# Moving half of the softmax scaling of some query tiles from GpSimd to VectorE

## The reference, cut to what matters

```
s = einsum('bqhd,bkhd->bhqk', qb, k) * scale
s = where(mask, s, NEG_INF)
p = softmax(s, axis=-1)            # layer one: a sink logit joins the denominator
o = einsum('bhqk,bkhd->bqhd', p, v)
# layer two: o = g[..., 0:1] * o_c + g[..., 1:2] * o_s + g[..., 2:3] * o_w
```

## Time and profile before

| what | value |
|---|---|
| time, median of 3 runs (lowest to highest) | 2753.47 us (2751.24 to 2755.43) |
| the profiled execution: its time | 2746.99 us |
| the profiled execution: span from first to last instruction | 2745.2 us |
| busy over the span | PE 88%, PEld 67%, DVE 58%, ACT 28%, POOL 33% |
| the chain that ended last, by engine | PE 60%, POOL 17%, DVE 14%, ACT 5%, issue 3% |
| mean granted clock of TensorE | 0.919 of full speed |

### The profile page before, as it was taken

How to read it: one execution, slowest core, us unless ns; L and a number is a source line. 1 busy time by engine, 2 the same in 40 slices (tenths; PEclk the granted TensorE clock), 3 DMA queues, 4 the chain that set the end, 5 groups by cost and what they waited for, 6 DMA issues and landing times.

```text
span 2745.2 us, 31261 instructions
## 1 busy us (share of the span) xinstructions
PE 2406.8 (88%) x12233; PEld 1831.3 (67%) x12233; DVE 1591.6 (58%) x2435; ACT 766.2 (28%) x1706; POOL 910.1 (33%) x944
## 2 busy tenths in 40 slices
PE   3968898689999899799879989899799998999978
PEld 2756676468887666676666857476477785747656
DVE  7676684753244665565654457683745536766463
ACT  2233212512001453324322152322311215232311
POOL 2873897378601346852020010400302001030120
PEclk7979898888689899899989989999999999999999
DMA  6440455044543001330111202021121120212111
GB/s 211 136 132 9 115 138 123 1 123 116 137 74 62 17 2 40 116 114 32 62 51 57 69 28 76 29 93 46 46 92 62 62 78 31 62 31 78 61 46 62
DMA packets 229157, 200.27 MB, mean 73 GB/s; under 512 B 86835, under 2 KB 213139, under 8 KB 228755
## 3 DMA queue, kind: packets, MB, share of 16 engines
q1 hardware_dynamic: 217491, 156.33, 20.6%
q0 software_dynamic: 11520, 41.95, 5.3%
HBM read 196.16 MB, written 2.10 MB: 72 GB/s over the span
## 4 chain that ended last, share of the span: by engine, by line
PE 60%; POOL 17%; DVE 14%; ACT 5%; issue 3%; DMA 0%; SPq 0%; DVEq 0%; ACTq 0%; POOLq 0%
PE bank L506 14%; PE bank L507 14%; PE bank L508 14%; POOL mix L2198 6%; POOL mix L2195 4%; PE bank L618 4%; PE bank L654 3%; DVE wring_parts L1496 2%; PE bank L632 2%; POOL mix L2201 2%; POOL mix L2182 2%; PE bank L818 1%; DVE bank L1567 1%; DVE whi_parts L1495 1%; PE bank L572 1%
## 5 line engine op out<-in xcount | busy, mean ns | idle before, releaser
L507 PE MATMUL bank<-h_parts,whi_parts 128*128 128x512 f32 (+2 forms) x1336 | 539.1, 404 | 0.0
L1496 DVE TENSOR_TENSOR wring_parts<-wring,whi_parts 128x2048 fp32r<-128x2048 f32 (+1 forms) x138 | 330.1, 2392 | 4.8
L1495 DVE CAST whi_parts<-wring 128x2048 fp32r<-128x2048 f32 (+1 forms) x138 | 195.1, 1414 | 196.8 <-PE bank L508 158.4
L507 PEld LDWEIGHTS bank<-h_parts,whi_parts 128*128 128x128 f32 (+2 forms) x1336 | 253.8, 190 | 69.9 <-issue 6.0
L2198 POOL TENSOR_TENSOR mix<-mix 128x512 f32<-128x512 f32 (+1 forms) x160 | 216.3, 1352 | 12.5
L506 PE MATMUL bank<-vt_parts,whi_parts 128*128 128x512 f32 (+2 forms) x472 | 199.6, 423 | 18.0 <-POOL h_parts L2229 12.1
L507 PE MATMUL bank<-mix_parts,whi_parts 128*128 128x512 f32 x512 | 204.1, 399 | 0.0
L506 PE MATMUL bank<-pt_parts,whi_parts 128*128 128x512 f32 x392 | 165.5, 422 | 31.1 <-DVE wring_parts L1496 16.2
L508 PE MATMUL bank<-vt_parts,wring_parts 128*128 128x512 f32 (+2 forms) x472 | 190.5, 404 | 0.0
L1567 DVE CUSTOM_DVE_ANT_0 bank<-bank,causal 128x128 f32<-128x128 f32 (+3 forms) x256 | 120.3, 512 | 75.5 <-PE bank L618 75.1
L2195 POOL TENSOR_TENSOR mix<-mix,cond 128x1024 f32<-128x1024 f32 x80 | 161.0, 2013 | 8.7 <-DMA mix<-in_ada_w 7.0
(11 more groups left out here) (372 smaller groups left out, 5347.5 us busy)
## 6 DMA issues: line engine op xcount, KB each, us to landing
wring<-in_w_in SPq DMA_DIRECT2D x60, 1024.0 KB, 5.2
mix<-in_ada_w POOLq DMA_DIRECT2D x80, 512.0 KB, 4.8
wring<-in_w_out SPq DMA_DIRECT2D x16, 1024.0 KB, 5.2
wring<-in_mla_w_in SPq DMA_DIRECT2D x10, 1024.0 KB, 7.1
wring<-in_mla_w_out SPq DMA_DIRECT2D x8, 1024.0 KB, 5.4
wring<-in_swa_w_in SPq DMA_DIRECT2D x32, 256.0 KB, 4.8
wring<-in_nsa_w_in SPq DMA_DIRECT2D x32, 256.0 KB, 4.6
wring<-in_nsa_w_in SPq DMA_DIRECT2D x6, 1024.0 KB, 6.0
```

The costliest lines, as they stand in the source:

```text
L507: pe.matmul(bank, lh, rl, start=False, stop=False)
L1495: chain(dve.tensor_copy(high, whole))
L1496: dve.tensor_tensor(low, whole, high.bitcast(F32), ALU.subtract).then_inc(done, 1)
```

## The change

In the first stack, VectorE now multiplies the second head's row in the steps that `scaled_by_dve` names: i = 3 in layers zero, two and three, and i = 1, 2 and 3 in layer one. GpSimd keeps the first head's row there, and both rows in all other steps. VectorE's multiplication stands in `row_sum`, right behind the reciprocal and ahead of the next `row_max`; it waits for the reciprocal through `rinv_ready`, and raises a new semaphore, `p_second`. That makes 4 such instructions in layer zero, 24 in layer one, 16 in layer two and 4 in layer three. The wait of `turn` is split as well: where the two heads have a bank each, the transposes of the first head wait only for the first head's row (this holds for i = 2 too), and those of the second for the second's. `row_factor` is the old computation of the factor, taken out as a function.

```
--- before.py
+++ after.py
@@ -269,7 +269,7 @@
         small_normed, lat_split = sem("small_normed"), sem("lat_split")
         w_split, mix_split, h_shifted, h_kept, out_half = sem("w_split"), sem("mix_split"), sem("h_shifted"), sem("h_kept"), sem("out_half")
         max_ready, sum_ready, rinv_ready, pool_step, p_ready = sem("max_ready"), sem("sum_ready"), sem("rinv_ready"), sem("pool_step"), sem("p_ready")
-        p_scaled, p_mixed, turn_full, turned_dve, turned_act = sem("p_scaled"), sem("p_mixed"), sem("turn_full"), sem("turned_dve"), sem("turned_act")
+        p_scaled, p_mixed, p_second, turn_full, turned_dve, turned_act = sem("p_scaled"), sem("p_mixed"), sem("p_second"), sem("turn_full"), sem("turned_dve"), sem("turned_act")
         dve_step, act_step = sem("dve_step"), sem("act_step")
         cmp_act, cmp_dve, cmp_pool, c_max, c_exp = sem("cmp_act"), sem("cmp_dve"), sem("cmp_pool"), sem("c_max"), sem("c_exp")
         gate_sig = sem("gate_sig")
@@ -443,6 +443,14 @@
                 return pr[:, j, j * P:]
             return raw[:, j, 4 + j * P:] if j < 2 else rs[:, 0:S - 2 * P] if j == 2 else rs[:, S - 2 * P:S - P]
 
+        def row_factor(L, u, i, s):
+
+            if L != 2:
+                return ones[:, 0:1]
+            b, br = u // 2, u % 2
+            c = 3 * (8 * (b // 4) + 4 * s + b % 4) + 1 + br
+            return gbr[:, i, c:c + 1]
+
         def sink_of(g, s):
             return g + SWA_G * s
 
@@ -458,6 +466,10 @@
         def on_dve(L, i, part):
 
             return L < 4 and (i < 2 or i == 2 and L != 1 and part[0] == 0)
+
+        def scaled_by_dve(L, i):
+
+            return L < 4 and (i == NT - 1 or L == 1 and i > 0)
 
         turns, turn_done, turn_count = {}, [], {True: 0, False: 0}
         for L in range(len(LAYERS) + L2):
@@ -622,8 +634,11 @@
 
                 def turn(m):
                     u, i = todo[m]
-                    pe.wait_ge(*(cnt(p_ready, 2) if L < 4 else cnt(p_mixed)))
                     for part in parts(L, i):
+                        if L >= 4:
+                            pe.wait_ge(*cnt(p_mixed))
+                        for s in part if L < 4 else ():
+                            pe.wait_ge(*cnt(p_second if s and scaled_by_dve(L, i) else p_ready))
                         n = turns[(L, m, part)]
                         if n >= 2:
                             pe.wait_ge(*turn_done[n - 2])
@@ -1571,6 +1586,12 @@
                     if L == 1:
                         chain(dve.tensor_tensor(stat_pair(1, m), stat_pair(1, m), stat_pair(3, m), ALU.add))
                     dve.reciprocal(stat_pair(2, m), stat_pair(1, m)).then_inc(rinv_ready, 1)
+                    u, i = todo[m]
+                    at = cnt(rinv_ready)
+                    if scaled_by_dve(L, i):
+                        dve.wait_ge(*at)
+                        p_ = rows_slot(m, 1)[:, 0:len(key_tiles(L, i)) * P]
+                        dve.tensor_scalar(p_, p_, stat_at(2, m, 1), row_factor(L, u, i, 1), ALU.mult, ALU.mult).then_inc(p_second, 1)
 
                 def mix_rows(m):
 
@@ -2215,12 +2236,8 @@
                             if s:
                                 pool.tensor_scalar(p_, p_, stat_at(2, m, s), lam[:, L - 4, 0:1], ALU.mult, ALU.mult).then_inc(p_scaled, 1)
                             continue
-                        factor = ones[:, 0:1]
-                        if L == 2:
-                            b, br = u // 2, u % 2
-                            c = 3 * (8 * (b // 4) + 4 * s + b % 4) + 1 + br
-                            factor = gbr[:, i, c:c + 1]
-                        pool.tensor_scalar(p_, p_, stat_at(2, m, s), factor, ALU.mult, ALU.mult).then_inc(p_ready, 1)
+                        if not (s and scaled_by_dve(L, i)):
+                            pool.tensor_scalar(p_, p_, stat_at(2, m, s), row_factor(L, u, i, s), ALU.mult, ALU.mult).then_inc(p_ready, 1)
 
             def low_parts(L):
```

## The result

The changed kernel takes 2760.94 us in the median of 22 runs, the kernel before 2754.18 us in the median of as many beside it. The ratio is 1.0023, with a 95% interval from 1.0015 to 1.0032: slower by 6.3 us (4.1 to 8.8). The prediction was 2763.5 us, a rise of 10.0. The execution that was profiled took 2751.31 us (span 2749.6) in place of 2746.99 (2745.2).

A forecast was written before the change was run, and what follows sets the result against it. Layer one was held bound by a VectorE-ScalarE loop without GpSimd; in layer two TensorE was busy 149.67 of 169.30 us. Terms 9.1 + 1.5 - 0.6 = +10.0 us gave a median of 2763.5 us, range +6 to +13 (2759.5 to 2766.5).

The forecast's parts named there:

- The cost of the multiply: VectorE's added instruction: 0.40 us for 256 columns, 0.54 for 512, starting 0.20 us after its reciprocal.
- Layer one: VectorE-ScalarE loop: 23 multiplies each delay the next maximum by 0.44 us, 10.1, less 1.0 soaked up: +9.1 us.
- no POOL: Layer one's chain of waits was said to hold no GpSimd work, so relieving GpSimd takes nothing out of the loop.
- Who is first: Race after the reciprocal: VectorE leads GpSimd by 0.06 us; the loser waits, then does nearly its whole work.
- The CASTs of the earlier trace: Evidence for the race: with a VectorE CAST 0.04 us ahead, GpSimd's instruction took 2.297 us where its like takes 1.080.
- the ends: Attention ends, layers zero to two: GpSimd through sooner after the last reciprocal (0.23 us in zero and two), together -0.6 us.
- Layer two: Last query tile's turns: a bank wait replaces the wait for GpSimd, 0.12 us later in 14 pairs, less 0.2: +1.5 us.
- The split wait for i = 2 moves little: Turns of i = 2: little effect, since TensorE seldom waits for these rows outside layer one; no size given.
- layers zero and three: Two turns each like layer two's, plus a last one that gains about 0.3 us in layer three: zero together.
- GpSimd first: Rival: GpSimd wins each race, delaying VectorE's multiply; about +30 us at most, range +18 to +32, chance 0.23.
- Soaked up: Rival: ScalarE's and TensorE's idle time takes half of the 0.44 us delay; +5 us, range -3 to +5.5, chance 0.13.
- The wait for GpSimd is worth what it shows: Rival: VectorE has room, so only the 21 waiting turns count, each gaining 0.23 to 0.77 us; -5 to -16, chance 0.06.

The follow-up runs named there:

- experiment 2: The changed kernel with VectorE scaling the second row of i = 3 in layers zero, two and three, none in layer one: 2755.48 us, ratio 1.0006 to before.
- experiment 3: The changed kernel with GpSimd scaling every row as before, so that only the wait of `turn` is split by head: 2748.48 us, ratio 0.9980 to before.
- experiment 7: The changed kernel with VectorE's multiply put behind the next maxima but ahead of the copies of the turned rows: 2755.29 us, ratio 0.9993 to before.
- experiment 4: The changed kernel with VectorE's multiply behind the next maxima and the copies, all four layers: 2739.84 us, ratio 0.9948 to before; run again, 2742.99 us, 0.9958.
- experiment 1: The changed kernel with VectorE scaling only in layer one (i = 1 to 3), split wait kept: 2756.0 us, ratio 1.0005 to before.
- experiment 6: The changed kernel with two tiny chained VectorE copies ahead of its multiply, so that GpSimd starts first: 2788.73 us, ratio 1.0119 to before.

## Why the prediction held, and where it didn't

- *The cost of the multiply* was 0.411 us for 256 columns and 0.546 for 512 (forecast 0.40 and 0.54), starting 0.20 behind the reciprocal (0.20). The maximum moved from +0.08 to +0.53 (forecast +0.52). Right.
- *Layer one*: +9.0 us between the two profiles (forecast +9.1). That its multiplies ahead of the maximum are the cause is shown by taking them away (experiments 2 and 3) and by moving them behind the maxima or the copies (7 and 4), where it falls back to 86 to 88 us. The two sizes in the sum were both off, and cancelled: a delay is 0.46 us and not 0.44, so 23 of them are 10.6, and 1.6 are soaked up and not 1.0. They are soaked up in four steps, in each of which the maximum stood 0.24 to 0.57 us behind its reciprocal already, waiting for scores. Two of them are those behind the weight splits, which grow by 0.05 us each. The chain went through GpSimd there, so "no POOL" was wrong for these two. Other profiles without the multiplies have more of such waits, and there the multiplies cost less, down to 6.2 us. That the two profiles agree with the forecast to 0.1 us is luck.
- *Who is first*: VectorE, with a lead of 0.07 us (0.06). But the size was off. I had GpSimd's row do its whole work behind the multiply, and end at +1.55. It took 1.04 us with 512 columns and ended at +1.31: 0.56 us behind the multiply's end, not 0.81. With VectorE first, it grows by 0.27 us (0.77 to 1.04) with 512 columns and by 0.14 (0.55 to 0.69) with 256, in place of "0.4 to 0.5". The CASTs of the earlier trace rows were the wrong measure for it. In the time this changes little, since TensorE waits for the copy all the same. Only the ends gain more: GpSimd goes on to the modulation 1.31, 0.92 and 1.30 us behind the last reciprocal of layers zero, one and two, in place of 1.78, 1.31 and 1.75. That is 1.3 us together, where the sum had 0.6.
- *Layer two*: +1.6 us (forecast +1.5), the wait for GpSimd replaced by one for the copy L1616, first head at +1.82 (1.71) and second head at +2.41 (2.34), behind ScalarE's copy, which ends at +2.30 (2.29). The sum and the mechanism of the bank waits were right, and the sentence "The split wait for i = 2 moves little" was where I stopped too early: I weighed the split for i = 2 and never priced it by itself for i = 3. There it is worth 5.6 us of layer two (experiment 3). The multiply ahead of the copy takes back 7.4 (experiment 2 less 3). So the +1.5 is the small difference of two effects that the forecast didn't have apart. In layers zero and three it is the same on a smaller scale: at a granted clock of 1.00 the stretch is 56.2 us before, 55.3 with the split wait alone and 56.5 after, so +0.3 each (forecast zero together).
- *The total*: the measured +6.3 us (4.1 to 8.8) lies under the +10.0, at the lower edge of the forecast's own range of 6 to 13. The ends are 0.7 us of the difference, and layers zero and three would make it 0.6 larger. The rest, some 3.6 us, can't be pinned to one term. It is likeliest in layer one. In the timed runs its multiplies add 0.25% or 6.9 us (experiment 1 less 3) and 0.17% or 4.7 us (the change less experiment 2), each uncertain by about 5, where the sum had 9.1. The stretches of the profile add up to +9.0 and +1.6, and layer zero's -1.6 goes with the clock in that profile.
- *The rivals*: GpSimd first did not happen. Its terms add up to 20 + 13 + 3 - 1.7 = +34 us and not to "about +30", so the range of the prediction left out its own upper end. "Soaked up" happened in part: of layer one's 10.6 us at least 1.6 go that way, and the measured total lies nearer to this rival's +5 than to +10.0, with an interval that holds both the rival's +5 and the forecast's lower part; only the profiles, with 0.46 us in nearly every step, speak against it as the main effect. "The wait for GpSimd is worth what it shows", -5 to -16 us, did not happen as the change stood. The turns of layer two did gain that way, 0.38 us each, but from the split wait, with or without the moved multiply behind the copies. That experiment 4 as a whole comes to -12 to -14 us doesn't bear the rival out, since part of it lies elsewhere.

Open: why the moved multiply gains more than its turns and ends show (experiment 4), and the rest of experiment 6 in layer two. Also, the same kernel's layer one took 85.9 and 88.0 us in its two profiles, at a granted clock of 0.88 and 0.81. Waits of the maxima for scores are 1.3 us of that; the rest I have not traced. It bounds what a single profile can say of layer one to about 2 us.

## What to carry to other kernels

Before giving a helper's work to an engine with slack, find the loop that this engine closes, and put the work behind the last instruction that someone waits for, where the engine would idle anyway; a multiply of 0.40 us cost 0.46 ahead of the maximum, and behind the copies nothing in two of three steps and 0.32 in the third. Price every part of a change by itself, even one that looks like an accessory: the split wait alone was a gain here (-5.5 us, 1.9 to 9.4), and the move of work undid it until it stood behind the copies. A wait that a list of waits shows as long is worth only what is not late next; read for each the instruction that would be waited for if it were gone.

## What the runs showed of the hardware

When VectorE and GpSimd scale a row each at the same time, the second to start takes longer, but by less than the time that they overlap. With VectorE first by 0.07 us GpSimd's 128x512 row took 1.04 us in place of 0.77, while VectorE's took its full 0.55; all sixteen rows agree:

```profile
L2240 POOL TENSOR_SCALAR rs<-rs,stat,gbr x16: 1040/1042/1043, 913.7 to 1076.2; 128x512 f32<-128x512 f32 x16
...
L1594 DVE TENSOR_SCALAR tmp<-tmp,stat,gbr x16: 545/546/547, 913.6 to 1076.1; 128x512 f32<-128x512 f32 x16
```

With GpSimd first by 0.26 us (experiment 7) or by 0.34 (experiment 6) it is VectorE's that grows, by 0.24 us and by 0.17, and GpSimd's that keeps its 0.77 or 0.78. The first one is not slowed by more than 0.02 us in any of these. The overlap, from the start of the second to the end of the first, goes with the price:

| first, columns | overlap, us | the second takes longer by |
|---|---|---|
| GpSimd, 512 (experiment 7) | 0.51 | 0.24 |
| VectorE, 512 (the change) | 0.48 | 0.27 |
| GpSimd, 512 (experiment 6) | 0.44 | 0.17 |
| VectorE, 256 (the change) | 0.34 | 0.14 |
| GpSimd, 256 (experiment 6) | 0.23 | 0.01 |

The price is the overlap less 0.20 to 0.27 us. The Trainium skill (SBUF — State Buffer, Who interferes with whom) has the loser blocked for the winner's whole instruction. Read as "it begins when the winner is through", that does not fit: the multiply of experiment 7 would have ended at 957.16 + 0.54 = 957.70, and it ended at 957.44. But these rows don't show that the two use the memory at once. If the second can do its first 0.2 us or so while it is held up, and only then has to wait, the same numbers come out; no run here separates the two. The CASTs of the earlier trace rows don't follow the same sum: there the second paid 1.22 us for an overlap of 1.18, and 0.25 for one of 0.39.
